# Stick-breaking attention beside dense layers: the turn of the weights goes behind the scores and values of its slot

## The reference

```python
def _sb_block(qb, qpos, k, v, kpos):
    z = jnp.einsum('bqhd,bkhd->bhqk', qb, k) * (SB_HEAD_DIM ** -0.5)
    mask = kpos[None, :] < qpos[:, None]
    log_beta = jax.nn.log_sigmoid(z)
    log_1m = jnp.where(mask, log_beta - z, 0.0)
    after = lax.cumsum(log_1m, axis=3, reverse=True) - log_1m
    a = jnp.where(mask, jnp.exp(log_beta + after), 0.0)
    return jnp.einsum('bhqk,bkhd->bqhd', a, v)

def _layer(x, ...):
    h = x @ w_in                       # q | k | v | u
    a_out = _stick_breaking(q, k_all, v_all, start_pos)
    p_out, new_pool = _pool_mix(u, pool_hist, start_pos, pool_w, pool_scale)
    x1 = _layer_norm(ALPHA * x + jnp.concatenate([a_out, p_out], -1) @ w_out, ln1_g, ln1_b)
    ffn = (silu(x1 @ w_gate) * (x1 @ w_up)) @ w_down      # inner width 2816
    return _layer_norm(ALPHA * x1 + ffn, ln2_g, ln2_b), k, v, new_pool
```

## Time and profile before

| what | value |
|---|---|
| runs before | 2710.47, 2711.99, 2713.18 us (median 2711.99) |
| the profiled execution | 2712.2 us, its span 2710.4 us |
| PE busy | 2608.0 us, 96% of the span |
| DVE, ACT, POOL busy | 1559.6, 1112.3, 1085.5 us |
| slots with attention | from about 140 to 280, 460 to 960, 1040 to 1400 and 1590 to 2080 us |

### The profile page before, as it was taken

How to read it: one execution, slowest core, us unless ns; L and a number is a source line. 1 busy time by engine, 2 the same in 40 slices (tenths; PEclk the granted TensorE clock), 3 DMA queues, 4 the chain that set the end, 5 groups by cost and what they waited for, 6 DMA issues and landing times.

```text
span 2710.4 us, 38792 instructions
## 1 busy us (share of the span) xinstructions
PE 2608.0 (96%) x14560; PEld 2232.5 (82%) x14560; DVE 1559.6 (58%) x2123; ACT 1112.3 (41%) x1903; POOL 1085.5 (40%) x949
## 2 busy tenths in 40 slices
PE   8998999999999999999999999999999999999997
PEld 8976788778877887788778887878878887999996
DVE  4467445777442346778763377887775354543335
ACT  3355424556322216555542155556554213222222
POOL 2344323655322216545642155555653214232222
PEclk9999999999999999999999999999999999999999
DMA  6687875675445524344336244334443622223222
GB/s 197 186 237 214 265 246 156 187 228 160 117 117 157 180 85 126 107 123 111 107 121 217 78 124 107 112 97 116 134 109 99 210 67 86 86 78 125 86 86 72
DMA packets 457799, 373.97 MB, mean 138 GB/s; under 512 B 29063, under 2 KB 390911, under 8 KB 457614
## 3 DMA queue, kind: packets, MB, share of 16 engines
q1 hardware_dynamic: 457614, 371.50, 45.7%
HBM read 303.33 MB, written 68.09 MB: 137 GB/s over the span
## 4 chain that ended last, share of the span: by engine, by line
PE 82%; DVE 7%; issue 4%; DMA 2%; ACT 2%; SPq 1%; POOL 1%; DVEq 0%; ACTq 0%; POOLq 0%
PE bank L1230 33%; PE bank L1274 18%; PE bank L1146 9%; PE bank L1087 7%; PE bank L996 4%; PE bank L1042 4%; PE bank L1012 4%; DVE left L1689 1%; DMA gw_lo_raw<-in_w_in_dram 1%; DMA mixT_scratch<-o_lo 1%; DVE aT L1680 1%; DVE stats L1702 1%; DVE later_lad L1873 1%; PE bank L1032 1%; PE bank L1110 1%
## 5 line engine op out<-in xcount | busy, mean ns | idle before, releaser
L1230 PE MATMUL bank<-x1T,gw_hi 128*128 128x512 f32 (+1 forms) x3488 | 931.2, 356 | 4.5 <-DVE hT_lo_raw L1773 3.0
L1230 PEld LDWEIGHTS bank<-x1T,gw_hi 128*128 128x128 f32 x3488 | 601.1, 189 | 84.7 <-issue 4.4
L1230 PE MATMUL bank<-x1T,gw_lo 128*128 128x512 f32 (+1 forms) x1744 | 615.0, 353 | 0.0
L2127 POOL TENSOR_TENSOR beta<-beta,left 128x512 f32<-128x512 f32 (+2 forms) x326 | 349.4, 1072 | 409.2 <-DVE left L1689 408.3
L2154 POOL TENSOR_TENSOR gw_lo<-gw_lo_raw,gw_hi 128x1024 fp32r<-128x1024 f32 x88 | 222.4, 2527 | 601.7 <-ACT gw_hi L1425 601.5
L1689 DVE TENSOR_TENSOR_SCAN left<-bank,left,zero_t 128x512 f32<-128x512 f32 (+2 forms) x326 | 363.6, 1115 | 71.4 <-ACT bank L1370 67.4
L1805 DVE TENSOR_TENSOR acc<-bank,acc 128x512 f32<-128x512 f32 x320 | 218.8, 686 | 269.8 <-PE bank L1274 269.5
L1146 PE MATMUL bank<-x1T,gw_hi 128*128 128x256 f32 (+2 forms) x1472 | 360.4, 337 | 8.4 <-POOL gw_lo L2167 4.8
L1360 ACT ACTIVATE aT<-bank 128x512 fp32r<-128x512 f32 (+2 forms) x326 | 173.7, 533 | 472.6 <-PE bank L1012 399.1
L1230 PEld LDWEIGHTS bank<-x1T,gw_lo 128*128 128x128 f32 x1744 | 329.1, 189 | 46.7
L1274 PE MATMUL bank<-dw_hi,hT_hi 128*128 128x512 f32 x748 | 304.9, 408 | 13.7 <-issue 7.5
(11 more groups left out here) (172 smaller groups left out, 3876.3 us busy)
## 6 DMA issues: line engine op xcount, KB each, us to landing
gw_lo_raw<-in_w_gate_dram SPq DMA_DIRECT2D x88, 512.0 KB, 4.0
gw_lo_raw<-in_w_up_dram SPq DMA_DIRECT2D x88, 512.0 KB, 4.1
dw_lo_raw<-in_w_down_dram SPq DMA_DIRECT2D x88, 512.0 KB, 4.4
gw_lo_raw<-in_w_in_dram SPq DMA_DIRECT2D x64, 512.0 KB, 4.8
k_st<-kT_scratch SPq DMA_DIRECT2D x160, 128.0 KB, 4.1
v_st<-v_scratch SPq DMA_DIRECT2D x80, 256.0 KB, 4.4
acc<-in_x_prompt_dram SPq DMA_DIRECT2D x32, 512.0 KB, 7.2
q_st<-qT_scratch SPq DMA_DIRECT2D x128, 128.0 KB, 4.1
```

The lines of the kernel that those rows point to most:

```text
L1230: m = pe.matmul(gu_bank(g, n)[:, 0:w], gw[L % 4][a][:, k, :], x1T[x][:, k, first:first + w], start=k == 0 and s == 0, stop=k == KD - 1 and ...
L2127: pool.tensor_tensor(x[:, 0:w], x[:, 0:w], left[n % RL][:, 1:w + 1], ALU.mult).then_inc(a_done, 1)
```

## The change

In `background`, PE made for each slot: the turn of the step before (and opening values), then scores and values of the step that is due. Now it makes: opening values of the step before, then scores and values of the step that is due, then the turn of the step before. The function `turning` is split in two, `late_values` and `turning`; nothing else differs, and no other engine's instructions move.

```diff
                 if lo <= lo + s - AT_TURN < hi:
                     turn(lo + s - AT_TURN)
+
+            def late_values(g, s):
+                lo, hi = SEGMENTS[g]
                 u = lo + s - AT_V
                 if lo <= u < hi and ITEMS[u].sample:
                     values(u, (3,))
...
                 for kind, g, s in due.get(slot - 1, ()):
                     if kind == ATTENTION:
-                        turning(g, s)
+                        late_values(g, s)
                 for kind, b, s in due.get(slot, ()):
                     (attention, mixing)[kind](b, s)
+                for kind, g, s in due.get(slot - 1, ()):
+                    if kind == ATTENTION:
+                        turning(g, s)
```

## The result

The changed kernel takes 2775.46 us (median of 4 runs, 2773.71 to 2778.4) beside 2712.27 for the kernel before on the same chip (2710.47 to 2713.18). The ratio is 1.0237, with a 95% interval of 1.0224 to 1.025: 63 us slower. The forecast was 2736 with a range of 2720 to 2754. The direction was right, the size was not. The time is near the 2772 of rival 3, "the delay is handed on"; whether its mechanism came too is told further down.

The account below looks back on a forecast made before the run. The prediction took PE, busy for 96% of the span, as the bound. Its terms 14 + 8 + 3 - 3.5 + 2.5 gave +24 us on 2712.2, so 2736 us, range 2720 to 2754.

Parts of the forecast that it names:

- rival 3: Late sigmoids and scans push work behind them into the next slots, or the clock dips often: about 2772 us; chance 0.11.
- What the change hangs on: ACT and DVE wait for PE's turn, which starts their copy, low part, sigmoids and scan; the slot's scores start nothing.
- Rivals 1 and 2: Scores and values fill the turn's waits, 2690 us, chance 0.05; ACT's idle time covers the delay, 2709 to 2716, chance 0.08.
- Term A: Lone turn after a moved one comes at 1.84 us but needs 2.11, a hole of 0.27: +14 us (5 to 20).
- Terms B and C: Scores wait for the scan: three steps in adjoining slots, about +8 us; moved turns that already wait, +3 us.
- Term C: Twelve moved turns that fill a wait; put behind, each adds its own 0.24 to 0.36 us: +3 us (0 to 5).
- Term D: Eight lone turns: opening values ahead fill the turn's wait for DVE, up to 0.45 each: -3.5 us (-5 to 0).
- Term E: Down products whose late low part gets later by 0.93 us, three or four places: +2.5 us (0 to 5).
- The clock: PE's granted clock may dip after long holes: put at 0, with -4 to +6 us kept for the range.
- What would show it: Predicted signs: PE's turn waits some 90, about 35 us; scores' waits over 10 us, mostly block 0; ACT's wait some 450.

## Why the prediction was wrong, by its steps

- **What the change hangs on** was right in this: the turn starts a chain through ACT and DVE, and the time came out slower. Rivals 1 and 2 fell: the scores do not start at once when put first.
- **Term A, the lone turn**: the mechanism and the distance of 2.11 came as said, with 90 places; the size was too small. The table's +16.0 holds terms A and D together, for which the prediction had +10.5. Without the turns with opening values it is about +21 for +14, just above the term's own bound of 20.
- **Terms B and C, the scores in slots with a moved turn**: this is the step that failed, by its count. Together they gave +11, from 13 and 12 places. The moved turns and the scores of their slots show +23.3 (39.9 - 16.6), from 54 places with a hole, and the waits of the scores read 36.8 us where "over 10" was said, in 41 places. This is the largest single part of what the sum lacks (39 us), but not all of it: some 12 us are missing here, 7 in term A, 7 in the clock, 5 behind the lone turns, and 8 or 9 in the rest that no row of the table has. "Most of the rise in block 0" was wrong too: ACT's copies of the turned rows fall behind by 4 us in block 0, 20 in block 1, 13 in block 2 and 27 in block 3.
- The reason for the low count can be read in rival 3, in the sentence used against it: "gaps of two slots behind each moved turn in blocks 2 and 3 give the chain 3.9 us for its 3.68". That chain was followed from the turn. The scores' chain does not begin there. It begins in the slot before theirs, with what DVE has to do ahead of the low part (a down sum of 0.69 at 1814.53; the sum of a head's output at 679.07 in block 1, last section), and at 1814.33 2.74 us stand against 2.31. The prediction went by the list of waits, in which the scores wait 14 times, and found twelve places; by the starts on PE there are 35. And it did not look at all for places where the turn's own 0.36 us was what covered the wait.
- **Term C's argument** (put behind, the turn adds its own width to the wait) was the right one, and the earlier trace rows the right rows. It held at 53 places: in 17 the wait was filled whole, and in 36 a hole was there already and grew by 0.35 us on average.
- **Term D**: right in sign, a little small: 5.0 us faster when tried alone, and about -5.0 in the holes of the changed kernel, for -3.5.
- **Term E**: the down products' waits for their hidden rows rose from 7.5 to 10.6 us, +3.1 for +2.5, as read; they were not tried by themselves.
- **The clock**: put at 0 with -4 to +6 kept; 7.3 us were lost, a little outside. In the kernel with half a scan, which has fewer long holes, the loss is 17.6 us instead of 30.1; but in the changed kernel with the sum behind the step, which is slower still (2796), it is 22.6. So the loss is not read off the sum of the holes; what sets it stays open.
- **What would show it**: PE's waits at the turn were to rise to some 90 and 35 us. The list of waits shows the opposite, 13 and 6.0, since it hides holes of 0.27; by the starts there are 96 and 30.1 us. ACT's wait before the copy was to grow by about 0.9 per moved turn, "to some 450". That last figure was a slip: 128 times 0.9 on top of 399 is 514. It grew by 128 to 527.5, 1.0 per moved turn.
- **Rival 3** came within 4 us of the time (2772), and that is in good part luck. Its 46 us were to come from 99 slots, through hidden rows, silu and down sums pushed into the next slots. The down products' own waits grew by 3.1 us; the scores of 54 slots and their turns gave 23.3, and its A was 7 short. What is borne out of it is that late work is handed on, here to the scores, and that the clock dips more.

## What to carry to other kernels

Before moving a piece of work off the front of a slot, compute for what stands behind it when its inputs are ready, also where the trace shows no wait, and take the distances from the starts and not from the list of waits. If the piece ends just as they arrive, it is a filler, and its whole length is at stake. Follow such a chain back through the producing engine's own queue order (what it must do first), not from the event that interests you. And when two consumers wait for one engine, an order that serves one sooner must be priced at the other.

## What the hardware showed that was not expected

**A DVE operation on two SBUF operands stands still beside POOL.** The sum of a head's output, 64x512, takes 0.68 or 0.69 us in 17 of its 32 instances in the changed kernel. At the longest of the 41 waits of the scores (the low part and the scan stand behind it):

```profile
678.99 2.38 POOL L2164 TENSOR_TENSOR dw_lo<-dw_lo_raw,dw_hi 128x1024 fp32r<-128x1024 f32 x1
...
679.07 2.85 DVE L1681 TENSOR_TENSOR o_t<-o_top,o_t 64x512 f32<-64x512 f32 x1
...
681.85 0.54 DVE L1686 TENSOR_TENSOR aT<-bank,aT 128x384 fp32r<-128x384 f32 x1
682.32 1.26 DVE L1695 TENSOR_TENSOR_SCAN left<-bank,left,zero_t 128x512 f32<-128x512 f32 x1
...
683.63 0.39 PE L996 MATMUL bank<-k_st,q_st 128*128 128x256 f32 x1 [3.07 <-DVE left L1695]
```

POOL began 0.08 us earlier, and DVE ends 0.55 after POOL does, a little less than its own 0.68. The other 15 instances take 0.76 to 2.85 us, and every one of them began while a POOL operation was running and ended 0.54 to 0.55 us after it. The low part of the hidden rows (two SBUF operands) takes 0.64 to 2.89 us, 18 of 86 over 0.70, all of them with the same 0.55 behind POOL, while the turned rows' low part, which reads one operand from PSUM, never takes over 0.69 in 326 instances. The Trainium skill, "SBUF — State Buffer", section "SBUF: two separate sides", says that DVE with two SBUF inputs and a GpSimd operation that reads SBUF take turns on a shared pair of ports and that the loser is blocked for the whole instruction; the trace agrees, with 2.85 us for 0.68. With the casts on POOL (87 of 2.51 us; one stayed on DVE) 34 of the 86 low parts of hidden rows in the changed kernel are drawn long instead of 18, and the waits for them grew by 12 us: a good part of why all three kernels became slower.

**Two holes of 0.8 us were followed by half clock, and one of 3.1 was not.** In the changed kernel the scores at 1734.26 waited 0.86 us and a turn of the feed-forward's input at 1736.13 waited 0.78; a product behind them is drawn with 0.63 us instead of 0.40:

```profile
1734.26 0.39 PE L996 MATMUL bank<-k_st,q_st 128*128 128x256 f32 x1 [0.86 <-DVE left L1695]
...
1736.13 1.31 PE L1116 MATMUL bank<-ident,acc 128*128 128x128 f32 x8 [0.78 <-issue]
...
1738.08 0.63 PE L1280 MATMUL bank<-dw_lo,hT_hi 128*128 128x512 f32 x1
```

The window of this stretch, with the granted clock (0.68, a part at 1.2 instead of 2.4 GHz) ahead of the last two numbers:

```profile
1735.00:1740.00 5.00, 4.15 (x16) 2.97 (x15) 3.01 (x6) 1.72 (x3) 0.86 (x4) 0.68 0.88 301
```

That is 1.6 us lost (5 x 0.32) behind 1.6 us of waiting; the prediction had thought of one hole of 3.4 us only. The longest wait of the scores, the 3.07 us that ended at 683.63, cost no clock:

```profile
680.00:685.00 5.00, 1.93 (x12) 1.42 (x11) 3.58 (x3) 0.26 (x2) 2.51 (x3) 1.00 0.45 112
685.00:690.00 5.00, 5.00 (x27) 4.14 (x25) 3.06 (x6) 3.30 (x9) 2.87 (x5) 1.00 0.50 121
```

So here the length of a hole alone did not tell whether the clock would fall; what does stays open.
